# A top-k threshold search whose candidate carries the sign, five masks ahead of the attention, and a rotary swap by transfers

## The chip, the cores and the metric

The program runs on one core of one Trainium2 chip. The core has a matrix engine (TensorE, PE), a vector engine (VectorE, DVE), a scalar engine (ScalarE, ACT), a general engine (GpSimd, POOL) and a queue engine (SyncE, SP); each takes its own instructions in order, and they meet at semaphores. The metric is the device time of one execution in microseconds (us), lower is better. Before the change it is 2630.7 us, the median of 3 runs.

## The reference

One inference step of a two-layer decoder for a prompt of 1024 tokens and 8 sequences of 4 new tokens each (32 tokens, 512 cached ones each), model width 1024. Only the first layer's sparse attention matters here:

```python
def partial_rope(x, cos, sin):           # first 16 of 64 head dims
    x1, x2 = x[..., :8], x[..., 8:16]
    return concatenate([x1 * c - x2 * s, x2 * c + x1 * s, x[..., 16:]])

def attn_project(h, w_in, pos):          # p = h @ w_in, 2120 columns
    q, k, v, qi, ki, wi = split(p, ...)  # q, k, qi, ki get partial_rope

def block(i):                            # 128 queries against 1024 keys
    sc = indexer_scores(qib, wib, ki, valid)   # sum_h relu(qi.ki) * wi
    _, sel = lax.top_k(sc, 256)                # exactly 256 keys a query
    return sparse_attend(qb, k[sel], v[sel])   # softmax over them
```

Every query attends to exactly its 256 best keys (129 of 516 for the sampled tokens), ties going to the earlier key. After it come the output projection, a SwiGLU block, a convolution layer and another SwiGLU block, all untouched by the change.

## The kernel before

Activations are held transposed (features on the 128 partitions, 1056 tokens along the row) and cut into three chunks of 352 tokens. Products are made nearly exact in float32 by splitting each operand into a high and a low part: one tile of a projection (128 output features, 352 tokens) is 24 matmuls, 8 blocks of 128 inputs by three products. The order of all instructions is written out by hand, engine by engine; there is no scheduler. The functions `sp_...`, `pe_...`, `act_...`, `dve_...`, `pool_...` are the programs of the engines, and `x.wait_ge(semaphore, value)` is where one waits for another.

The part in question has four stages.

- **First projection stage** (`pe_proj_a`): five blocks of 3 tiles: the indexer's keys and weights (block 0, 64 or 72 rows), then the indexer's queries. Tile r goes through a chain: PE makes it, ACT evicts it to `psgA` (`act_evac_rope`), PE multiplies it by the permutation `rotm` that exchanges the two halves of each rotated group (`pe_rot`), DVE multiplies that result in PSUM by the sine table into `pafA`, POOL multiplies `psgA` by the cosine table (`pool_cos`), DVE adds (`dve_rope`, counted on `fin_rdy`). `psgA` and `pafA` have two buffers each. POOL also makes the low parts of the weights (`proj_lo`). After tiles 9, 11, 12 and 13 PE turns pages of cached indexer keys (`pe_turn_kx`), which SP has loaded into `xr` by 32 transfers.
- **Index stage**: scores of queries against keys into `s_all`, one row of 384 to 1024 keys for each of the query tiles 2 to 7 (tiles 0 and 1 have no more than 256 keys), and `s_smp` for the 32 sampled tokens.
- **Second projection stage** (`pe_proj_b`), 39 items on PE: 3 tiles of keys, 9 value tiles (`v_tok`), 27 more rotary tiles (1 block of keys, 8 of queries), with a chunk of the modulation weights (`pe_chunks`, about one an item, loaded by SP into a ring of four slots) after each, and the K copy of `pe_turn_k` in nine of them. Here ACT evicts the rotated copy as well (`act_rot`), and POOL does sine product, cosine product and sum (`pool_fin`). At the same time DVE looks for the 256th largest score of every row: a binary search over the bits of a float. One round counts, for seven rows of scores at once, how many values reach the candidate, and sets one bit of the threshold by it. DVE counts five of them, ACT the two longest (1024 and 896 keys) with a Sign activation (`act_count`). Where ACT does so is fixed in its program: the table `COUNT_AT` lays each half round at the middle or end of an item of PE's, by times in which an item counts 10 units (a value item 7).
- **Attention** (`dve_att` and others): 64 pairs (query tile, pair of heads), pair n uses tile n // 8. DVE adds the tile's mask to the scores and takes the row's extreme (`dve_min`), ACT makes the exponential, POOL divides, PE turns and multiplies by the values. The masks of tiles 2 to 7 and of the sampled tokens are made of the thresholds by DVE, six steps each (`dve_mask_step`), 1.5 steps a pair in the first 28 pairs (`dve_masks_at`). Forty chunks of modulation weights are multiplied here as well (`pe_pair_chunks`).

The search before works on magnitudes: a row whose threshold is negative is multiplied by -1 first (`sig`), so that the searched value is positive, and multiplied back at the first step of its mask.

## Time and profile before

| | |
|---|---|
| median of 3 runs | 2630.7 us (2629.48 to 2631.83) |
| the profiled execution, its own time | 2635.32 us |
| its span, first to last instruction | 2633.5 us |
| mean granted TensorE clock | 0.983 |
| busy: PE, DVE, ACT, POOL | 95%, 67%, 42%, 49% |
| chain that ended last, by engine | PE 70%, DVE 11%, DMA 6%, issue 5%, POOL 4%, ACT 2% |
| first projection stage, index stage, second projection stage, attention | about 50 to 131, 131 to 185.6, 185.6 to 382.5, 382.5 to 650 us |

The profiled execution lies 4.6 us above the median, so differences worked out from its rows are taken off the median. The four stages are the first quarter of the kernel; what follows (650 us on) is bound by PE and starts when the attention has ended, so it moves as one block.

In the rows further down a timeline row gives the start in us, the time that the group took in us, the engine (PEld is the load of weights into PE, SPq is SP's queue of transfers), line, operation, what is written from what, the shapes, the number, and in brackets how long the engine had been idle before it and for whom it waited. A row of the stretches view gives for each engine the busy us and the number of instructions, then PE's granted clock as a share of full, the share of the transfer engines, and GB/s. A row of the view by line gives the total busy us, the mean ns of one, and the idle time before.

### The profile page before, as it was taken

What the parts mean: (1) busy time and instruction counts of PE and PEld (TensorE: products, weight loads), DVE (VectorE), ACT (ScalarE), POOL (GpSimd) and SP (SyncE); (2) the same over time, 40 slices, a digit from 0 to 9 for tenths busy, and PEclk for the clock granted to TensorE, in tenths of its full rate; (3) what the DMA queues carried; (4) which work ended last, traced back from release to release, by engine and by line L of the source; (5) the groups of instructions that cost most, each with busy time, mean ns of one, the idle gap of its engine ahead of it and who ended that gap; (6) DMA issues with size and microseconds to landing.
All of it is one profiled execution on the core that took longest, in us unless ns stands there. A gap on an engine that the chain in (4) does not pass through costs nothing.

```text
span 2633.5 us, 51699 instructions
## 1 busy us (share of the span) xinstructions
PE 2512.0 (95%) x20164; PEld 2312.3 (88%) x20164; DVE 1771.3 (67%) x3137; ACT 1101.9 (42%) x2061; POOL 1287.4 (49%) x967
## 2 busy tenths in 40 slices
PE   6979999999998999999999989999989999999999
PEld 4848874677798999999999989999989999999999
DVE  6388888665347756656567687767785665656775
ACT  5155656775235444344212343332454444442223
POOL 3404652344134656566544545545455656654454
PEclk7999999999999999999999999999999999999999
DMA  9205557201433435344894333328334534469731
GB/s 322 78 21 153 177 207 255 70 2 68 129 113 101 146 124 164 117 155 139 328 349 167 117 98 106 107 82 328 117 98 131 164 117 155 139 207 366 278 131 70
DMA packets 316390, 408.00 MB, mean 155 GB/s; under 512 B 40816, under 2 KB 227032, under 8 KB 313338
## 3 DMA queue, kind: packets, MB, share of 16 engines
q1 hardware_dynamic: 316154, 404.75, 45.9%
q8 instruction: 161, 2.64, 0.4%
q14 instruction: 75, 0.61, 0.1%
HBM read 284.85 MB, written 119.85 MB: 154 GB/s over the span
## 4 chain that ended last, share of the span: by engine, by line
PE 70%; DVE 11%; DMA 6%; issue 5%; POOL 4%; ACT 2%; SPq 2%; ACTq 0%; DVEq 0%; POOLq 0%
PE PS L595 10%; PE PS L2492 9%; PE PS L2494 9%; PE PS L2493 9%; PE PS L2553 5%; PE PS L2555 5%; PE PS L2556 5%; PE PS L1855 3%; PE PS L1884 2%; PE PS L1866 2%; POOL ring L2864 2%; DMA t_scratch<-stage 2%; DMA a_scratch<-stage 1%; POOL stage L2877 1%; DVE s_all L1552 1%
## 5 line engine op out<-in xcount | busy, mean ns | idle before, releaser
L2492 PE MATMUL PS<-th,ring 128*128 128x264 f32 x2800 | 800.2, 286 | 19.9 <-DVE y L3007 8.2
L2494 PE MATMUL PS<-th,ring 128*128 128x264 f32 x2800 | 796.8, 285 | 0.0
L2493 PE MATMUL PS<-th,ring 128*128 128x264 f32 x2800 | 795.9, 284 | 0.0
L2492 PEld LDWEIGHTS PS<-th,ring 128*128 128x128 f32 x2800 | 527.8, 189 | 26.8 <-issue 26.1
L2493 PEld LDWEIGHTS PS<-th,ring 128*128 128x128 f32 x2800 | 528.0, 189 | 0.0
L2494 PEld LDWEIGHTS PS<-th,ring 128*128 128x128 f32 x2800 | 527.9, 189 | 0.0
L2864 POOL TENSOR_TENSOR ring<-wraw,ring 128x512 fp32r<-128x512 f32 x232 | 340.3, 1469 | 368.1 <-ACT ring L2648 367.8
L2864 POOL TENSOR_TENSOR ring<-sums,ring 128x512 fp32r<-128x512 f32 x216 | 322.2, 1493 | 276.3 <-ACT ring L2648 276.3
L2553 PE MATMUL PS<-th,ring 128*128 128x264 f32 x1232 | 354.8, 288 | 14.3 <-DVE zs L3196 6.7
L2555 PE MATMUL PS<-th,ring 128*128 128x264 f32 x1232 | 352.9, 286 | 0.0
L2556 PE MATMUL PS<-th,ring 128*128 128x264 f32 x1232 | 352.5, 286 | 0.0
L2648 ACT ACTIVATE ring<-wraw 128x512 fp32r<-128x512 f32 x340 | 211.8, 626 | 299.2 <-PE PS L2556 168.2
L3193 DVE SCALAR_TENSOR_TENSOR y<-PS,mod,y 128x528 f32<-128x528 f32 x308 | 235.0, 766 | 141.2 <-PE PS L2556 128.0
L3007 DVE TENSOR_TENSOR y<-y,PS 128x528 f32<-128x528 f32 x150 | 104.9, 699 | 293.8 <-PE PS L2494 293.6
L2648 ACT ACTIVATE ring<-sums 128x512 fp32r<-128x512 f32 x216 | 136.1, 631 | 353.2 <-PE PS L2494 173.3
L2553 PEld LDWEIGHTS PS<-th,ring 128*128 128x128 f32 x1232 | 234.4, 190 | 16.1 <-issue 11.7
L2556 PEld LDWEIGHTS PS<-th,ring 128*128 128x128 f32 x1232 | 234.7, 191 | 0.0
L2555 PEld LDWEIGHTS PS<-th,ring 128*128 128x128 f32 x1232 | 234.6, 190 | 0.0
L2877 POOL TENSOR_TENSOR stage<-y,stage 128x528 fp32r<-128x528 f32 x110 | 179.2, 1629 | 77.3 <-ACT stage L2668 77.3
L595 PE MATMUL PS<-hhi,uhi 128*128 128x352 f32 (+1 forms) x552 | 189.0, 342 | 14.5 <-DVE hlo L1267 7.3
L2696 ACT ACTIVATE y<-PS 128x528 f32<-128x528 f32 x173 | 105.1, 607 | 186.4 <-PE PS L2494 185.3
L595 PE MATMUL PS<-hhi,ulo 128*128 128x352 f32 (+1 forms) x552 | 180.8, 328 | 0.0
(393 smaller groups left out, 5164.4 us busy)
## 6 DMA issues: line engine op xcount, KB each, us to landing
t_scratch<-stage SPq DMA_DIRECT2D x154, 528.0 KB, 3.3
th<-t_scratch SPq DMA_DIRECT2D x77, 1056.0 KB, 8.7
wraw<-in_ffn_w_gu_dram SPq DMA_DIRECT2D x96, 512.0 KB, 5.2
wraw<-in_ada_w_dram SPq DMA_DIRECT2D x80, 512.0 KB, 4.8
wraw<-in_ffn_w_down_dram SPq DMA_DIRECT2D x80, 256.0 KB, 5.9
wraw<-in_conv_w_in_dram SPq DMA_DIRECT2D x28, 512.0 KB, 5.3
y<-y_scratch SPq DMA_DIRECT2D x12, 1056.0 KB, 8.9
y_scratch<-y SPq DMA_DIRECT2D x6, 2112.0 KB, 7.9
```

What stands on the lines that cost most here:

```text
L595: last = pe.matmul(out, w(kt), x(kt), start=(n == 0), stop=(n == 3 * count - 1))
L2492: pe.matmul(out, hi, x[:, TH, k, :], start=(k == 0 and i in (1, 2, 5)), stop=False, skip_group_check=True)
L2493: pe.matmul(out, hi, x[:, TL, k, :], start=False, stop=False, skip_group_check=True)
L2494: last = pe.matmul(out, lo, x[:, TH, k, :], start=False, stop=(k == 3), skip_group_check=True)
L2553: pe.matmul(out, hi, x[:, TH, 2 * k + s, :], start=(k == 0 and i in (1, 2, 5)), stop=False, skip_group_check=True)
L2555: pe.matmul(out, hi, x[:, TL, 2 * k + s, :], start=False, stop=False, skip_group_check=True)
L2556: last = pe.matmul(out, lo, x[:, TH, 2 * k + s, :], start=False, stop=(k == 1), skip_group_check=True)
L2648: act.activation(slot_of(p)[:, RH, :], split_source(p), ACT.Copy).then_inc(w_hi, 1)
L2696: act.activation(out, result(r, it.groups), ACT.Silu if it.kind == "g" and pos == 6 else ACT.Copy).then_inc(rd_a, 1)
L2864: pool.tensor_tensor(w[:, RL, :], split_source(p), w[:, RH, :].bitcast(F32), ALU.subtract).then_inc(w_lop, 1)
L2877: pool.tensor_tensor(lo.rearrange("p (s n) -> p s n", s=2), token_part(v, i), hi.rearrange("p (s n) -> p s n", s=2), ALU.subtract).then_in ...
L3193: ins = dve.scalar_tensor_tensor(out=out, in0=result(r, BOTH), scalar=gate_of(f, m)[:, 0:1], in1=out, op0=ALU.mult, op1=ALU.add)
```

## The change

It has three parts. (1) The rotary halves are exchanged by transfers from SBUF to SBUF that ACT issues (`act_swap`): four of 8 partitions by 352 numbers a tile (two in block 0), from `psgA` or `psgB` into rows of `pafA` or `pafB` that were set to zero once. PE's 45 products by `rotm` and ACT's 30 evictions of them are gone. (2) The search sets the sign first: one count at 0 gives every row a start of +2 or about -2, the 31 bits below are toggled into `cand` by exclusive or, and there is no separate threshold. The multiplications by the sign before the search and in each mask are gone, and 31 rounds are left of 32. `COUNT_AT` starts at 13 units in place of 24, with 4.8 a half round in place of 4.9. (3) Five of the seven masks (tiles 2, 3, 4, 5, 6, of 384 to 896 keys) are made by DVE ahead of its first instruction of the attention, in `relu` as scratch; the masks of tile 7 and of the sampled tokens follow at pairs 2 to 13, a step a pair.

```diff
-    return [next(s for s, t in enumerate(at) if t >= 24 + 4.9 * h) for h in range(64)]
+    return [next(s for s, t in enumerate(at) if t >= 13 + 4.8 * h) for h in range(62)]
...
         def dve_start(dve):
             dve.memset(ones[:], 1.0)
+            dve.memset(pafA[:], 0.0)
...
-        def pe_rot(pe, r):
-            rows = P if r >= 3 else 64
-            pe.wait_ge(evac, rope_m(r) + 1)
-            after(pe, ts_rdy, r - 1)
-            src = (psgA if r < 15 else psgB)[0:rows, r % 2, :]
-            pe.matmul(rot_bank(r)[0:rows, 0:CH], rotm[0:rows, 0:rows], src, start=True, stop=True).then_inc(rot_mm, 1)
+        def act_swap(act, r):
+
+            act.wait_ge(evac, rope_m(r) + 1)
+            after(act, fin_rdy, r - 1)
+            if r in (15, 16):
+                act.wait_ge(pm_rdy, 1)
+            src, dst = (psgA, pafA) if r < 15 else (psgB, pafB)
+            for head in (0,) if r < 3 else (0, 64):
+                for o in (head, head + 8):
+                    of = 2 * head + 8 - o
+                    act.dma_start(dst[o:o + 8, r % 2, :], src[of:of + 8, r % 2, :]).then_inc(swapped[r % 2], 16)
...
             act.wait_ge(up_mm, UP_END[p] - 2 + n)
-            after(act, rot_mm, r - 1)
+            swap_done(act, r - 2)
             after(act, qc_rdy, r - 1)
...
-        def act_rot(act, r):
-
-            act.wait_ge(rot_mm, r + 1)
-            after(act, fin_rdy, r - 1)
-            act.activation(pafB[:, r % 2, :], rot_bank(r)[:, 0:CH], ACT.Copy).then_inc(ts_rdy, 1)
...
                 for n in range(NCH):
                     act_evac_rope(act, 5, n, psgB)
                     act_count(act, 2 * (ITEM_AT[5] + n))
-                if n:
-                    act_rot(act, R_AT[5] + n - 1)
+                act_swap(act, R_AT[5] + n)
                 act_chunks(act, ITEM_AT[5] + n)
...
-            dve.wait_ge(rot_mm, r + 1)
-            after(dve, fin_rdy, r - 1)
-            dve.tensor_tensor(pafA[0:rows, r % 2, :], rot_bank(r)[0:rows, 0:CH], ropeS[0:rows, chunk(n)], ALU.mult)\
+            if r == 0:
+                dve.wait_ge(const_loaded, 48)
+            swap_done(dve, r)
+            dve.tensor_tensor(pafA[0:rows, r % 2, :], pafA[0:rows, r % 2, :], ropeS[0:rows, chunk(n)], ALU.mult)\
...
+            with dve.Fori(0, ROUNDS) as i:
+                dve.wait_ge(sel, i * 6 + base)
+                count(2, None, ALU.is_ge)
+                dve.wait_ge(cand_rdy, i + 1)
+                signal(count(6, None, ALU.is_lt))
+                count(3, None, ALU.is_ge)
+                count(4, None, ALU.is_ge)
+                signal(count(5, None, ALU.is_ge))
+                dve.wait_ge(sel, i * 6 + (base + 1))
+                dve.wait_ge(sign_cnt, i * NA + NA)
+                signal(dve.tensor_tensor(v(lt, 0, 3), v(cnt, 0, 3), v(kk, 0, 3), ALU.is_gt))
...
             if step == 0:
-                link(dve, dve.tensor_scalar(s, s, bv[0:rows, BS + 3 * E + j:BS + 3 * E + j + 1], None, ALU.mult))
                 link(dve, dve.tensor_scalar(A, s, t, 0.0, ALU.is_gt, ALU.add, accum_out=n))
...
+        MASKS_FIRST, MASKS_LATE = (2, 5, 4, 3, 1), (0, 6)
+
+        def dve_masks_first(dve, entries):
 
+            for j in MASKS_FIRST:
+                for step in range(6):
+                    dve_mask_step(dve, entries, j, step, relu)
             dve.wait_ge(ki_stored, 32)
...
-            for x in range(3 * n // 2, 3 * (n + 1) // 2 if n < 28 else 0):
-                dve_mask_step(dve, entries, (2, 5, 4, 3, 1, 0, 6)[x // 6], x % 6)
+            if 2 <= n < 2 + 6 * len(MASKS_LATE):
+                dve_mask_step(dve, entries, MASKS_LATE[(n - 2) // 6], (n - 2) % 6, mscr)
```

ACT in the second projection stage, the first two tiles of block 10, before (L1005 is the eviction, L900 a count, L1012 the eviction of the rotated copy, L828 the high part of a weight, L1026 the K copy):

```order
L1005 ACTIVATE psgB<-PS 128x352
L900 ACTIVATE junkA,bv<-s_all,bv 128x896
L1012 ACTIVATE pafB<-PS 128x352
L828 ACTIVATE uhi<-wraw 128x1024
L1026 ACTIVATE ktok<-PS 128x256
L900 ACTIVATE junkA,bv<-s_all,bv 128x1024
L1005 ACTIVATE psgB<-PS 128x352
L900 ACTIVATE junkA,bv<-s_all,bv 128x896
L1012 ACTIVATE pafB<-PS 128x352
L1026 ACTIVATE ktok<-PS 128x256
```

and the same two tiles after the change (L1000, L906, L827 and L1016 are the same statements under new line numbers, L855 is the swap):

```order
L1000 ACTIVATE psgB<-PS 128x352
L906 ACTIVATE junkA,bv<-s_all,bv 128x1024
L855 DMA pafB<-psgB 8x352 x4
L827 ACTIVATE uhi<-wraw 128x1024
L1016 ACTIVATE ktok<-PS 128x256
L906 ACTIVATE junkA,bv<-s_all,bv 128x896
L1000 ACTIVATE psgB<-PS 128x352
L906 ACTIVATE junkA,bv<-s_all,bv 128x1024
L855 DMA pafB<-psgB 8x352 x4
L1016 ACTIVATE ktok<-PS 128x256
```

The copy of the tile before (one activation) has given way to the swap of this tile (four transfers, issued by ACT in its own order).

DVE at the end of a round of the search, before (`junkC` is the count of the sampled tokens, 128x5 the five rows that DVE counts):

```order
L1600 TENSOR_SCALAR junkC,bv<-s_smp,bv 32x516
L1660 REGISTER_ALU
L1636 TENSOR_TENSOR PS<-bv,PS 128x5
L1662 REGISTER_ALU
L1638 TENSOR_SCALAR PS<-PS,bv 128x5
L1664 REGISTER_ALU
L1640 SCALAR_TENSOR_TENSOR bv<-PS,bv 128x5
L1645 TENSOR_TENSOR bv<-bv,PS 128x5
L1647 REGISTER_ALU
```

and after the change, from the wait for ACT's counts to the end of the round:

```order
L1626 TENSOR_TENSOR PS<-bv,PS 128x3
L1627 REGISTER_ALU
L1628 ISA
L1628 TENSOR_SCALAR PS<-bv 128x4
L1629 REGISTER_ALU
L1630 TENSOR_SCALAR PS<-PS,bv 128x3
L1631 REGISTER_ALU
L1632 ISA
L1632 SCALAR_TENSOR_TENSOR bv<-PS,bv 128x4
L1634 REGISTER_ALU
L1635 SCALAR_TENSOR_TENSOR bv<-PS,bv 128x3
L1616 REGISTER_ALU
```

Before, a round had eight small instructions, four for ACT's two rows among the counts and four for the others behind them; now it has five, all behind the last count.

DVE behind the search, before (L1682 is the last step of the search, L1942 the first of the attention):

```order
L1680 TENSOR_TENSOR PS<-PS,bv 128x2
L1681 TENSOR_TENSOR bv<-bv,PS 128x2
L1682 TENSOR_TENSOR bv<-bv 128x7
L1942 ISA PbS,bv<-PS,cneg 128x128
L1942 ISA bv 128x1
```

and after the change, the first of the five masks (35 instructions in all, then the attention):

```order
L1655 TENSOR_TENSOR bv<-bv,PS 128x2
L1666 TENSOR_SCALAR relu,bv<-s_all,bv 128x384
L1668 TENSOR_SCALAR bv<-bv 128x1
L1669 TENSOR_SCALAR relu<-s_all,bv 128x384
L1671 SCALAR_TENSOR_TENSOR relu<-relu 128x384
L1673 SCALAR_TENSOR_TENSOR relu<-relu,bv 128x384
L1675 SCALAR_TENSOR_TENSOR relu<-s_all,bv,relu 128x384
L1677 TENSOR_SCALAR masks<-relu 128x384
```

## Rows read from the trace of the kernel before

**Rows 1.** Stretches: second projection stage and first 28 pairs, busy us of each engine.

```profile
185.60:382.50 196.90, 194.72 (x1344) 162.53 (x1344) 175.76 (x636) 111.58 (x223) 101.75 (x96) 0.98 0.51 158
...
382.50:475.00 92.50, 82.92 (x767) 41.27 (x768) 74.61 (x233) 56.11 (x200) 29.05 (x57) 0.94 0.78 260
```

**Rows 2.** PE's timeline: a tile without a rotation behind it, and rotations.

```profile
236.64 0.43 PE L595 MATMUL PS<-hhi,uhi 128*128 128x352 f32 x1
...
241.23 0.43 PE L595 MATMUL PS<-hhi,uhi 128*128 128x352 f32 x1
...
353.57 0.75 PE L849 MATMUL PS<-psgB,rotm 128*128 128x352 f32 x2
...
358.74 0.75 PE L849 MATMUL PS<-psgB,rotm 128*128 128x352 f32 x2
```

**Rows 3.** Timeline at the end of the first projection stage.

```profile
125.99 0.46 ACT L1005 ACTIVATE psgA<-PS 128x352 f32<-128x352 f32 x1 [4.43 <-PE PS L595]
...
127.21 0.63 DVE L1098 TENSOR_TENSOR qiT<-qcA,pafA 128x352 f32<-128x352 f32 x1
...
127.47 2.57 POOL L834 TENSOR_TENSOR ulo<-wraw,uhi 128x1024 fp32r<-128x1024 f32 x1
...
128.41 2.01 DVE L1098 TENSOR_TENSOR qiT<-qcA,pafA 128x352 f32<-128x352 f32 x1
```

**Rows 4.** The pages in `xr`: SP's queue, landing, PE's loads (ns; first and last start).

```profile
77.16 19.18 SPq L777 DMA_DIRECT2D xr<-in_cache_kidx_dram  x16
...
DMA to landing us min/median/max: 1.6/1.8/11.5
...
L924 PEld LDWEIGHTS PS<-ident,xr x16: 140/141/143, 102.1 to 121.7; 128*128 128x128 f32 x16
```

**Rows 5.** DVE's timeline, from the index stage into the search.

```profile
187.66 1.22 DVE L1600 TENSOR_SCALAR_CACHE_REDUCE junkA<-s_all 128x1024 bf16<-128x1024 f32 x1
...
193.22 0.53 DVE L1610 TENSOR_SCALAR PS<-bv 128x1 f32<-128x1 f32 x7
...
199.37 0.61 DVE L1600 TENSOR_SCALAR_CACHE_REDUCE junkB<-s_all,bv 128x384 bf16<-128x384 f32 x1
```

**Rows 6.** DVE's timeline, one round of the search.

```profile
231.56 0.61 DVE L1600 TENSOR_SCALAR_CACHE_REDUCE junkB<-s_all,bv 128x384 bf16<-128x384 f32 x1
...
235.66 0.17 DVE L1636 TENSOR_TENSOR PS<-bv,PS 128x5 f32<-128x5 f32 x1
...
236.54 0.61 DVE L1600 TENSOR_SCALAR_CACHE_REDUCE junkB<-s_all,bv 128x384 bf16<-128x384 f32 x1
```

**Rows 7.** Groups by line and shape of ACT, second projection stage.

```profile
L900 ACT ACTIVATE junkA<-s_all,bv 128x1024 bf16<-128x1024 f32 x32 | 36.8, 1150 | 41.0 <-DVE bv L1640 41.0
...
L900 ACT ACTIVATE junkA<-s_all,bv 128x896 bf16<-128x896 f32 x32 | 33.1, 1033 | 0.0
...
L828 ACT ACTIVATE uhi<-wraw 128x1024 fp32r<-128x1024 f32 x8 | 8.3, 1054 | 0.0
...
L1026 ACT ACTIVATE ktok<-PS 128x256 f32<-128x256 f32 x8 | 3.1, 382 | 0.5 <-DMA out_dram<-ktok 0.5
```

**Rows 8.** SP's queue: a small transfer at the start.

```profile
4.58 0.30 SPq L635 DMA_DIRECT2D vst<-in_c_prompt_dram  x1
```

**Rows 9.** Timeline from the last round to the attention.

```profile
373.84 0.18 DVE L1670 SCALAR_TENSOR_TENSOR bv<-bv 128x2 f32<-128x2 f32 x1
...
384.18 0.29 DVE L1942 CUSTOM_DVE_ANT_0 PbS<-PS,cneg 128x128 f32<-128x128 f32 x1
...
382.97 0.49 PE L1855 MATMUL PS<-kT,hhi 64*128 64x128 f32 x4 [0.54 <-ACT mod L889]
```

**Rows 10.** Groups by line and shape: two of the masks' instructions.

```profile
L1699 DVE TENSOR_TENSOR_SCAN mscr<-mscr 128x896 f32<-128x896 f32 x1 | 2.0, 2025 | 0.0
...
L1705 DVE TENSOR_SCALAR masks<-mscr 128x384 bf16<-128x384 f32 x1 | 0.4, 360 | 0.0
```

**Rows 11.** Waits in the first 28 pairs: who waited for whom.

```profile
PE PS L1866 <- POOL PbS L2023: 3.3, 5, 1.2
```

More of the change, by code:

```diff
@@ L893, in act_count @@
         def act_count(act, half):
-            for h in range(64):
+            for h in range(62):
                 if COUNT_AT[h] == half:
@@ L1018, in act_proj_a @@
                         act_evac_rope(act, p, n, psgA)
+                    act_swap(act, 3 * p + n)
                 proj_hi(act, p + WR)
@@ L1616, in dve_select @@
-            link(dve, ins)
-            for j, (s, rows, L, k) in enumerate(entries):
-                if j < NA:
-                    dve.tensor_scalar(ka[:, j:j + 1], one(kk, j), -2.0, float(L), ALU.mult, ALU.add)
-                dve.tensor_scalar(s, s, one(sig, j)[0:rows], None, ALU.mult)
-            ins = dve.memset(v(cand), 2.0)
+            ins = dve.tensor_tensor(v(cand), v(cand), v(th), ALU.add)
             link(dve, ins)
```

168 lines of the change are left out of this document (66 added, 102 removed).

## The prediction, written before the changed kernel ran

> **What bounds the kernel now.** I read the chain that ended last first: 70% PE, 11% DVE. The change touches only the first quarter, so I followed the chain there by stage. In both projection stages it is made of PE's tiles; the stretches view gives PE 194.7 busy of 196.9 us in the second one, and DVE 175.8 beside it [rows 1]. So two things run side by side from 185.6 on: PE's 39 items, and DVE's search, whose 32 rounds end at 373.8, followed by a closing part until 384.18. PE had its first scores under way at 382.97 and waited for DVE [rows 9]. **The attention starts when the later of the two is done, and before the change they are level within about a microsecond**: to gain, both must become shorter, and what is put on DVE ahead of the attention counts in full once DVE is the later. In the first 28 pairs PE is idle 92.5 - 82.9 = 9.6 us [rows 1], 3.3 of it named as POOL, which waits for DVE, busy with masks [rows 11].
>
> **First projection stage.** A rotation costs PE what an item with one takes above one without: 358.74 - 353.57 = 5.17 against 241.23 - 236.64 = 4.59, so 0.58 us [rows 2]. Fourteen of the fifteen rotations of this stage lie ahead of its end: 14 x 0.58 = 8.1 us off PE. Two things give some back.
> The pages in `xr` come from SP, which waits for nothing here that moves: its last transfer is issued by 77.16 + 19.18 = 96.34 and lands 1.8 later, at 98.1 [rows 4]. PE turned the first page at 102.1 [rows 4]; nine rotations earlier this is 96.9, so PE waits 1.2 us.
> The tail: the eviction of tile 14 started at 125.99, the sum of its rotary parts ended at 128.41 + 2.01 = 130.42, 4.4 us later [rows 3]. Now: eviction 0.46, four issues on ACT, the landing, DVE's product and sum. I find no transfer issued by ACT here; the nearest row is SP's of 8 partitions, 0.30 [rows 8]; I add 0.05 between two (an estimate), so 1.4 for four. Landing 1.8 [rows 4]. The last product could then start 3.7 us after the eviction began. But rows 3 show a sum of two SBUF operands taking 2.01 us and ending 0.4 after POOL's 2.57 us split ended (127.47 + 2.57 = 130.04), where the same sum took 0.63 just before it: DVE with two SBUF operands waits for POOL. The product used to read PSUM; now it reads SBUF twice and can wait too. POOL's split follows ACT's high part, which stands behind the four issues: 0.4 + 1.4 + 1.05, so it lies at 2.9 to 5.4, and product and sum end at 5.4 + 0.5 + 0.65 = 6.6. The tail grows 2.2 us (0.5 if the product gets in first).
> The Trainium skill (SBUF — State Buffer, "SBUF: two separate sides") says the port pair is an exclusive lock between a DVE operation with two SBUF inputs and a GpSimd one; by it the tail is the 6.6, which this case's 2.01 us sum agrees with.
> Stage gain: 8.1 - 1.2 - 2.2 = 4.7. The index stage moves as a block; none of its instructions change.
>
> **The search, from the start of the second projection stage (185.6).** Setup: seven counts at 187.66 to 193.2, then 6.2 us of sign factors until the first round at 199.37 [rows 5]. After: the same counts and about ten instructions of one to seven numbers, 0.07 to 0.17 each, 1.2 us in all. 5.0 us less; rounds could begin 8.8 after the stage's start.
> A round: 236.54 - 231.56 = 4.98 when it waits for nothing; 4.1 to 235.66 are five counts and what is done among them, 0.88 the last four small steps [rows 6]. Taking the four small steps of ACT's rows out from among the counts leaves 3.6 for these, and the new chain of five, two of them side by side, is some 0.65: 4.25 a round. But ACT's two counts stand at fixed places in PE's items, so DVE can't outrun PE: 9.6 units a round, an item of 10 units taking 4.59, or 4.8 with a K copy. PE paces the search.
> PE's stage: 196.9 - 30 x 0.58 = 179.5. By `COUNT_AT` the last half round (61) lies at 305.8 units, in item 33; behind this item's tile come five items and a chunk, 5 x 4.59 + 0.8 = 23.8, so the tile ends at 155.7. With eviction 0.4, count 1.03 [rows 7] and 0.8 for DVE's last steps: 158.
> **Does ACT keep up?** An item now: eviction 0.4, counts (1.15 + 1.03) x 10/9.6 = 2.3, K copy 0.38, a third of a high part 0.35 [rows 7], together 3.4; four issues 1.4; sum 4.8, against 4.6 to 4.8 for PE. That is level. Bounds: at no cost for an issue ACT has 1.2 us to spare; at 0.6, twice rows 8, it has 5.8 and is late by 1.2 an item. I take 0.35 because a swap is nearest in shape to the 8-row transfer of rows 8, and 1.5 us of lateness over some twenty rotary items that carry counts: last round at 159.5. Before it ended 373.8 - 185.6 = 188.2 after the start.
> A page has a price where no row has one: the Trainium skill (DMA: Bandwidth & Descriptors, "Anatomy of one DMA — SWDGE (gpsimd) path") puts the sequencer's own part of a transfer at about 50 ns. By it ACT would never be late and the end would come 1.5 us earlier than my sum; no run here shows it yet.
> Where the swap is late, POOL waits: it needs it only behind the next tile's cosine product, an item later, so 4.6 us cover 1.4 of issue, 1.8 of landing and a count of 1.15. Without the cover each late microsecond reaches ACT's eviction two tiles on.
>
> **Behind the search.** Closing part: 384.18 - 373.84 = 10.3 [rows 9]; the same eight passes over the two longest rows, one small step less: 10.2. Then the five masks, 35 instructions, the longest the scan of 896 keys, 2.03, the shortest of full width the last step of 384 keys, 0.36 [rows 10]; by shape, without the sign product, 3.7 + 4.5 + 5.4 + 6.1 + 6.9 = 26.7, and 0.04 between each and the next makes 28.1. DVE is ready at 159.5 + 10.2 + 28.1 = 197.8, where it was 384.18 - 185.6 = 198.6: a gain of 0.8. PE is done 18 us earlier than that and idles. The search's 29 us are eaten by the masks; PE's 17 us in this stage are hidden.
> **Attention.** It starts 4.7 + 0.8 = 5.5 earlier. In it POOL's 3.3 go, and some of the rest, since the queries and the first chunks have landed long before; two masks remain in pairs 2 to 13, one with a scan of 1024 keys, longer than that of rows 10, and take some back. I take 3.5 (bounds 0 and 9.6). The clock is left out: in this stage it was granted at 0.94 before [rows 1], and PE idles ahead of it in both kernels, now longer, which is one more reason not to take more.
> **Sum**: 5.5 + 3.5 = 9.0 off the profiled 2635.3, so off the median: 2630.7 - 9.0 = **2621.7 us**. What differs by under 0.2% (5.3 us) this measurement can't tell from no change.
>
> **Rivals.**
> *A, ACT hardly notices the swaps* (issues run beside its counts, and the product gets in ahead of POOL): 1.5 and 1.7 less, and more of the 9.6: some 2616. For it: waits and issues aren't counted as busy on any engine. Chance 0.25; the forecast itself 0.36.
> *B, ACT becomes the bound.* Its program is in order: counts, eviction and four issues; at 0.5 us an issue an item takes 5.4, 0.8 more than PE's, over twenty items 16 us in place of 1.5: 2636, slower. It decides from 1.5 + 9 us of lateness, 0.5 an item, some 0.45 an issue on. Against it: SP's 0.30; for it: SP does nothing else than issue, ACT's case isn't measured. Chance 0.18.
> *C, masks and sums wait for POOL.* The masks ahead run beside POOL's rotary work; fifteen of their 35 instructions read SBUF twice, as the sum of rows 3 did. At 0.45 us each (an estimate, a quarter of the 1.63 that the sum of rows 3 waited) it is 7 us: 2628, no change. Chance 0.14.
> *D, late landings.* The slowest landing in rows 4 is 11.5 us, with the queue full; ACT's swaps share the transfer engines, 51% busy in this stage [rows 1]. Ten swaps late by 2 us are 20 us: 2640. Against it: median 1.8. Chance 0.05.
> *E, nothing moves*: ACT level but attention gives nothing, 2626. Chance 0.02.
> From these: forecast and A 0.61 faster (a few of their cases fall short of 5.3, some of C beyond it), same 0.17, slower 0.22. Low end: A with all of the 9.6, 2612. High end: B, between its 2636 and 2644 at 0.6 us an issue: 2640.
>
> **What the profile of the changed kernel would show.** PE tiles of 3.8 us back to back in the first stage, a wait for `xr` of about 1 us at the first page; relu's last activation near 180.9 in place of 185.6; rounds of 4.4 to 4.6; ACT's queue with issues of about 0.35 and no idle time before its counts; PE ready some 18 us before DVE's first instruction of the attention, near 378.7; few waits for POOL behind it. Wrong would be: issues above 0.45; rounds of 5 or more; DVE's masks stretched beside POOL; an attention that takes as long as before.

## The result and the profile after

The changed kernel takes **2653.4 us** (median of 4 runs, 2650.3 to 2656.8), the kernel before beside it 2631.3 us (2629.5 to 2635.0): a ratio of 1.0073, 95% interval 1.0051 to 1.0095 (the ratio is the measurement's own estimate over all runs; the two medians alone give 1.0084). By the medians it is 22 us slower, where I forecast 9 us faster; the time lies above the high end of my range. The profiled execution took 2656.81 us (span 2655.0, mean granted clock 0.975 in place of 0.983).

The chain that ended last, shares of the span by engine; PE had 70% before, and issue 5%:

```profile
PE 62%; DVE 11%; issue 8%; DMA 6%; POOL 5%; SPq 3%; ACT 3%; ACTq 1%; DVEq 0%; POOLq 0%
```

Stretches from the end of the index stage to DVE's first minimum of the attention, and the 93 us behind it; they answer to [rows 1]:

```profile
182.40:401.20 218.80, 179.97 (x1288) 153.78 (x1288) 190.56 (x551) 100.18 (x192) 107.58 (x99) 0.92 0.53 166
401.20:494.20 93.00, 88.76 (x789) 44.59 (x790) 47.10 (x186) 57.51 (x203) 27.94 (x56) 0.89 0.68 221
```

The stage that I wanted at 197.8 us up to DVE's readiness takes 218.4. PE's busy time in it did fall, from 194.7 to 180.0 us: the rotations are gone. But PE is hardly earlier. Who PE and DVE waited for in this stretch (us in total, times, longest):

```profile
PE PS L1831 <- DVE bv L1918: 22.5, 1, 22.5
PE PS L868 <- DMA wraw<-in_ada_w_dram: 8.7, 5, 3.6
PE PS L594 <- ACT ktok L1016: 5.8, 8, 1.3
```

```profile
DVE PS L1626 <- ACT junkA L906: 10.4, 12, 2.5
```

PE's tiles of the stage end hardly sooner after its start than before (its first scores at 378.43 lie 195.6 us after 182.8; before, 382.97 lay 197.4 after 185.6; my working had 179.5), and then it stands 22.5 us until DVE is ready. ACT's transfers, from the view of their line (min/median/max in ns, first and last start):

```profile
L855 ACTq DMA_DIRECT2D pafB<-psgB x120: 631/632/1536, 189.1 to 376.2; - x120
```

An issue takes 0.632 us of ACT's queue, twice the 0.30 of [rows 8]. What that does depends on where it stands. ACT's timeline, one item of the K stretch:

```profile
304.80 1.15 ACT L906 ACTIVATE junkA<-s_all,bv 128x1024 bf16<-128x1024 f32 x1 [0.38 <-DVE bv L1635]
304.86 1.29 ACTq L855 DMA_DIRECT2D pafB<-psgB  x2
...
306.18 1.29 ACTq L855 DMA_DIRECT2D pafB<-psgB  x2
307.59 1.06 ACT L827 ACTIVATE uhi<-wraw 128x1024 fp32r<-128x1024 f32 x1 [1.55 <-PE PS L594]
308.56 0.37 ACT L1016 ACTIVATE ktok<-PS 128x256 f32<-128x256 f32 x1
308.82 1.03 ACT L906 ACTIVATE junkA<-s_all,bv 128x896 bf16<-128x896 f32 x1
...
309.85 0.45 ACT L1000 ACTIVATE psgB<-PS 128x352 f32<-128x352 f32 x1
```

The first count of a round runs at 304.80, two issues start right beside it, two more follow, then a high part and a K copy, and only at 308.82 comes the second count of the same round. The whole swap stands between a round's two counts. DVE's timeline, one round from 347.47 and, from 352.44, the last one, answers to [rows 6]:

```profile
347.47 0.61 DVE L1593 TENSOR_SCALAR_CACHE_REDUCE junkB<-s_all,bv 128x384 bf16<-128x384 f32 x1 [0.41 <-issue]
...
351.08 0.15 DVE L1626 TENSOR_TENSOR PS<-bv,PS 128x3 f32<-128x3 f32 x1
351.31 0.23 DVE L1628 TENSOR_SCALAR PS<-bv 128x4 int32<-128x4 f32 x1
351.44 0.22 DVE L1630 TENSOR_SCALAR PS<-PS,bv 128x3 int32<-128x3 f32 x1
351.68 0.22 DVE L1632 SCALAR_TENSOR_TENSOR bv<-PS,bv 128x4 int32<-128x4 int32 x1
351.82 0.21 DVE L1635 SCALAR_TENSOR_TENSOR bv<-PS,bv 128x3 int32<-128x3 int32 x1
352.44 0.61 DVE L1593 TENSOR_SCALAR_CACHE_REDUCE junkB<-s_all,bv 128x384 bf16<-128x384 f32 x1 [0.41 <-issue]
...
357.12 0.82 DVE L1641 SCALAR_TENSOR_TENSOR PS<-bv 128x2 f32<-128x2 f32 x1
```

Five small steps take 0.95 us bare, and the next count starts 0.41 us after them. The round from 347.47 waited for nothing, and the pitch to the next one is 4.97, what it was before. Then DVE's row from the closing part, the first instruction of the first two masks, and the attention's first (it was at 384.18, [rows 9]):

```profile
359.40 1.86 DVE L1650 TENSOR_TENSOR relu<-relu,s_all 128x1024 f32<-128x1024 f32 x1
...
369.25 0.61 DVE L1666 TENSOR_SCALAR_CACHE_REDUCE relu<-s_all,bv 128x384 f32<-128x384 f32 x1
...
375.60 0.75 DVE L1666 TENSOR_SCALAR_CACHE_REDUCE relu<-s_all,bv 128x512 f32<-128x512 f32 x1
...
401.20 0.29 DVE L1918 CUSTOM_DVE_ANT_0 PbS<-PS,cneg 128x128 f32<-128x128 f32 x1
```

| from the profiled executions | before | forecast | after |
|---|---|---|---|
| second projection stage starts (relu ends) | 185.6 | 180.9 | 182.8 |
| from there to the first round | 13.8 | 8.8 | 8.6 |
| from there to the last round's end | 188.2 | 159.5 | 174.2 |
| closing part | 10.3 | 10.2 | 12.2 |
| masks ahead | 0 | 28.1 | 32.0 |
| DVE's first minimum | 384.2 | 378.7 | 401.2 |
| from it to the first minimum of 640 keys | 104.2 | 100.7 | 103.2 |
| all, own time | 2635.3 | 2626.3 | 2656.8 |

The attention starts 17.0 us later, its stretch up to the first minimum of 640 keys is 1.0 shorter, and 5.5 more are lost behind that: PE ran at half clock once more in the output projection. PE's windows of the changed kernel (busy, count, clock, transfers' share, GB/s):

```profile
381.00:401.00 20.00, 0.00 (x0) 0.50 0.44 164
401.00:420.00 19.00, 15.96 (x100) 0.50 0.43 140
420.00:440.00 20.00, 18.86 (x174) 0.95 0.82 265
690.00:703.00 13.00, 12.34 (x88) 0.57 0.45 125
```

At 0.5 the clock is at its lower level, 1.2 GHz. It stayed there from PE's idle stretch until about 420, for 19 us of work; before, 384 to 394 had 0.62 and 394 to 404 had 0.87. After 690, behind a stretch in which PE's work has gaps in both kernels, it fell once more; before it did not.

Neither loss of clock can be put down to the longer idle time, though. The second fall is there in kernels in which PE never idled long ahead of the attention, here the kernel of e12 below, and so are 5.5 us behind the first minimum of 640 keys: that remainder was 2147.0 us before, 2152.4 in the changed kernel, and 2140.5 to 2156.1 in the experiments below (e1 2140.5, e12 2152.8, e8 2156.1; e5 left out). So what follows the attention did not move quite as one block.

```profile
670.00:690.00 20.00, 17.19 (x113) 0.66 0.44 123
```

And the low clock around the attention's start ended 9 to 14 us behind its first minimum in the kernel before and in eleven of the experiments, 21 in the changed kernel, and 23 to 24 in e1, e4 and e7. In e13 PE had idled 24.6 us ahead of it, more than the changed kernel's 22.5; in e1 and e4 it had waited for DVE 1.3 and 0.7 us.

### The profile page after: what moved, and what is told of

It reads as the page before. It is cut to its first block, busy times and chain, and to the rows that moved or that the text cites. A ratio compares the mean times of both kernels' runs of the same rounds, so it can differ in the third digit from the quotient of the medians.

```text
span 2655.0 us, 51486 instructions
## 1 busy us (share of the span) xinstructions
PE 2491.5 (94%) x20074; PEld 2301.6 (87%) x20074; DVE 1768.7 (67%) x3001; ACT 1089.5 (41%) x2027; POOL 1294.2 (49%) x968
## 3 DMA queue, kind: packets, MB, share of 16 engines
q8 instruction: 160, 2.62, 0.4%
## 4 chain that ended last, share of the span: by engine, by line
PE 62%; DVE 11%; issue 8%; DMA 6%; POOL 5%; SPq 3%; ACT 3%; ACTq 1%; DVEq 0%; POOLq 0%
PE PS L2468 9%; PE PS L2470 8%; PE PS L2469 8%; PE PS L2529 5%; PE PS L2531 5%; PE PS L2532 5%; PE PS L594 4%; PE PS L1831 3%; PE PS L1860 3%; DMA t_scratch<-stage 3%; PE PS L1842 2%; POOL ring L2840 2%; POOL stage L2853 2%; DMA a_scratch<-stage 1%; PE PS L2490 1%
## 5 line engine op out<-in xcount | busy, mean ns | idle before, releaser
L2468 PE MATMUL PS<-th,ring 128*128 128x264 f32 x2800 | 800.3, 286 | 22.5 <-DVE y L2983 8.0
L594 PE MATMUL PS<-hhi,uhi 128*128 128x352 f32 (+1 forms) x552 | 187.7, 340 | 20.5 <-DVE hlo L1257 7.4
L2672 ACT ACTIVATE y<-PS 128x528 f32<-128x528 f32 x173 | 105.2, 608 | 188.2 <-PE PS L2470 187.7
```

What stands on the lines that cost most here:

```text
L594: last = pe.matmul(out, w(kt), x(kt), start=(n == 0), stop=(n == 3 * count - 1))
L2468: pe.matmul(out, hi, x[:, TH, k, :], start=(k == 0 and i in (1, 2, 5)), stop=False, skip_group_check=True)
L2672: act.activation(out, result(r, it.groups), ACT.Silu if it.kind == "g" and pos == 6 else ACT.Copy).then_inc(rd_a, 1)
```

## The experiments

The search alone and the swap alone are the changed lines of one part put into the kernel before, or taken back out of the changed one. Masks are moved by one line, shown for e4 and e14:

```diff
-        MASKS_FIRST, MASKS_LATE = (2, 5, 4, 3, 1), (0, 6)
+        MASKS_FIRST, MASKS_LATE = (), (2, 5, 4, 3, 1, 0, 6)      # e3, e4, e9, e15
+        MASKS_FIRST, MASKS_LATE = (2,), (5, 4, 3, 1, 0, 6)       # e14
```

with 1.5 steps a pair inside the attention, from pair 0 on as before the change (in e14, and in e10 with its two masks ahead, from pair 2 on). The count table is one number:

```diff
-    return [next(s for s, t in enumerate(at) if t >= 13 + 4.8 * h) for h in range(62)]
+    return [next(s for s, t in enumerate(at) if t >= 13 + 4.96 * h) for h in range(62)]
```

Each experiment ran beside the kernel before (2634.6 to 2635.7 us there; 2631.3 beside the changed kernel). Differences in us between two experiments are taken from their ratios. "Start" is DVE's first minimum in the profiled execution, 384.2 before.

| | swap | new search | masks ahead | COUNT_AT | start | ratio, 95% |
|---|---|---|---|---|---|---|
| e1 | yes | no | 0 | as before | 377.6 | 0.9998, 0.9988 to 1.0009 |
| e3 | no | yes | 0 | 13 + 4.8 h | 383.2 | 0.9990, 0.9979 to 1.0001 |
| e2 | no | yes | 5 | 13 + 4.8 h | 398.4 | 1.0045, 1.0028 to 1.0063 |
| e4 | yes | yes | 0 | 13 + 4.8 h | 380.7 | 0.9993, 0.9980 to 1.0005 |
| changed kernel | yes | yes | 5 | 13 + 4.8 h | 401.2 | 1.0073, 1.0051 to 1.0095 |
| e9 | yes | yes | 0 | 13 + 4.96 h | 370.4 | 0.9955, 0.9940 to 0.9971 |
| e14 | yes | yes | 1 | 13 + 4.96 h | 371.5 | 0.9956, 0.9942 to 0.9970 |
| e13 | yes | yes | 5 | 13 + 4.96 h | 395.0 | 1.0036, 1.0023 to 1.0048 |
| e15 | no | yes | 0 | 13 + 4.96 h | 384.4 | 0.9990, 0.9975 to 1.0005 |

**First set: each part alone.** Theories: ACT's issues (I), against the search's rounds and the bare masks (L).

> The kernel before with the rotation by four small transfers a tile alone; search, COUNT_AT and masks are those of before. What the changed kernel's trace showed: first stage 3.2 us shorter (relu's last start 182 in place of 185.6), each issue 0.64 us on ACT, PE's second stage no shorter than before (379.2 - 182.4 = 196.8). Theory I (ACT's issues, 2.6 us a tile, hold up PE through its K copies and the search through ACT's counts): PE's items of the K stretch 5.2 to 6.1 us, rounds 5.3 us in the mean, attention starts at 378 to 382, time 2624 to 2630, so about no change. Theory L (issues hardly matter, the loss of 22 us comes from the search's rounds and the masks): PE's items 4.6 to 4.8 throughout, PE ready by 366, attention starts when the search ends, 182.4 + 13.8 + 32 x 4.98 + 10.3 = 366 to 368, time about 2614.

> The kernel before with the new search and the five masks ahead, the rotation left on PE. Theory L (a round of the new search takes 4.97 us on DVE as before, closing 12.2, masks 32 bare): rounds end near 185.6 + 9 + 31 x 5.05 = 351, attention starts at 395, eleven us later than before, time 2641 to 2646 (the upper end if PE's idle stretch costs clock again behind it). If the round were really 4.25 us and only ACT's issues had hidden it, rounds would follow PE's items (9.6 units of 0.517 = 4.96 a round), the same end: this run can't tell those two apart, its round without a wait for ACT can: 4.97 or 4.25. If the masks ahead were the gain that I had forecast behind the search (few waits for POOL, 3.5 us), the stretch from the first pair to the first mask of 640 keys falls from 104.2 to about 100.7.

> The kernel before with the new search alone: rotation on PE, all seven masks inside the attention as before, in the same order and rhythm. DVE ready 351 + 12.2 = 363, PE at 383: the attention starts with PE, at 383. Expected by theory L: time within 2 us of before (2630), DVE idle some 20 us ahead of the attention. A gain of over 4 us would say that DVE's small work in the attention got cheaper (the sign product gone), a loss that the new search costs something outside its own place.

> The changed kernel with none of the masks ahead of the attention: all seven inside it, in the rhythm of before. DVE ready at 357.0 + 12.2 = 369.2, PE at 379.2: the attention starts at 379.5, 22 us earlier than in the changed kernel. If the masks ahead are the whole loss: 2653.4 - 22 + 1 = 2632, and another 5 less if the stretches of half clock (401 to 420 and 690 to 703 in the changed kernel) go with PE's long idle: 2627. If it stays above 2640, something that I haven't named costs.

The masks carry the loss: e2 (2646.8 us, 0.8 above the range expected for it) against e3 starts 15.2 us later, the changed kernel against e4 20.5, and the times follow (0.55% and 0.80%, 14.5 and 21 us). The swap alone brings nothing, though it starts the attention 6.6 us earlier; the search alone brings nothing that can be told from no change.

Theory I, as I had put it, did not hold: in e1, with the same 0.632 us issues, PE's items of the K stretch take 4.8 to 5.1 us but for one of 6.0, not the 5.2 to 6.2 of the changed kernel. ACT in e1:

```profile
292.34 1.15 ACT L906 ACTIVATE junkA<-s_all,bv 128x1024 bf16<-128x1024 f32 x1
...
293.49 0.44 ACT L1000 ACTIVATE psgB<-PS 128x352 f32<-128x352 f32 x1
293.83 1.03 ACT L906 ACTIVATE junkA<-s_all,bv 128x896 bf16<-128x896 f32 x1
293.96 1.29 ACTq L855 DMA_DIRECT2D pafB<-psgB  x2
...
295.28 1.29 ACTq L855 DMA_DIRECT2D pafB<-psgB  x2
296.68 0.38 ACT L1016 ACTIVATE ktok<-PS 128x256 f32<-128x256 f32 x1 [1.72 <-issue]
```

Here the swap stands between the second count of one round (293.83) and the first of the next. That is where I then looked.

Part of e1's 6.6 us went with the clock. PE had waited 7.3 us for a chunk of weights just ahead of the attention, and the 20 us behind:

```profile
380.00:400.00 20.00, 17.10 (x104) 0.50 0.80 271
```

Its stretch of the first pairs took 107.7 us, 3.5 more than before. The rest of the 6.6 is not found in this trace, which was the fastest of e1's 12 runs (2625.8 against a median of 2634.2). The mean clock of the 12 was 0.979, that of the 29 runs of before 0.983, and among those 29 a clock lower by 0.001 went with 1.24 us more (correlation 0.79 in size): by that slope, an estimate, the difference is some 5 us.

**Second set: issues, the candidate's place, SP's queue.** Edits against e4:

```diff
# e5: each transfer of 8 rows as two of 4
+                    for q in (0, 4):
+                        act.dma_start(dst[o + q:o + q + 4, r % 2, :], src[of + q:of + q + 4, r % 2, :])
# e6: the step on the rows that ACT counts stands ahead of the last two counts
+                signal(dve.tensor_tensor(v(lt, 0, 3), v(cnt, 0, 3), v(kk, 0, 3), ALU.is_gt))
                 count(4, None, ALU.is_ge)
...
# e7: a step's chunks of weights ahead of its stores
-                    sp_chunks(sp, lo, lo + 3)
+                    sp_chunks(sp, lo, hi if p > 8 else lo + 3)
```

> The changed kernel without masks ahead (e4), but each swap of 8 rows made as two of 4 rows: eight issues a tile, the same bytes. Theory I (ACT pays by the issue, 0.64 us each): 5.1 us of issues a tile, an ACT item of 3.4 + 5.1 = 8.5 less about 1.2 that runs beside its counts, so items of some 7 us in the K stretch and rounds near 7 us there; over 27 rotary items that carry counts 2 us and more each on e4's 5.2: 2675 to 2700. If ACT pays by rows or bytes (an issue of 4 rows 0.32 us), nothing changes against e4's 2633.

Ratio 1.0291 (1.0274 to 1.0307), 2712.4 us, beyond what I expected. The issues of 4 rows:

```profile
L856 ACTq DMA_DIRECT2D pafB<-psgB x240: 584/585/617, 210.9 to 455.8; - x120
```

Half the bytes cost 0.585 us in place of 0.632: ACT pays nearly all of it by the issue. All 348 are 204 us of ACT's queue, where e4's 174 were 110: 94 us more, and 79 us came out in the time; the first stage alone grew by some 20 us (relu's last start at 203.7).

> e4 with the round's small steps in the places that they had before the change: the decision for the two rows that ACT counts (and the samples' row) between the fourth and last counts, not behind all five. Theory C (the new round gives ACT its candidate at its very end; ACT then stands in order ahead of its count, 35.4 us in e4, and evictions, K copies and swaps stand behind it, which stretches PE's items of the K stretch to 5.1 to 6.2 us, while the search of before with the same swaps had 4.8): ACT's waits for DVE under 20 us, K items 4.8 to 5.0, rounds 4.8 to 4.9, DVE through its closing part by 362 to 365 (369 in e4). PE's end gains 3 to 5 of its 12 lost unless loads hold it; time 2628 to 2632. Theory I (it is the issues as such): items stay at 5.2 to 6.2, time as e4.

A miss: ratio 1.0043 (1.0025 to 1.0061), 13 us slower than e4. Rounds of the K stretch took 5.8 to 7.1 us. DVE's timeline, two rounds of it, the decision on ACT's rows:

```profile
272.43 0.17 DVE L1624 TENSOR_TENSOR PS<-bv,PS 128x3 f32<-128x3 f32 x1 [0.90 <-ACT junkA L906]
...
279.53 0.17 DVE L1624 TENSOR_TENSOR PS<-bv,PS 128x3 f32<-128x3 f32 x1 [2.19 <-ACT junkA L906]
```

With the decision early, DVE stands still for ACT's second count with two counts of its own still to do, where in e4 it does them meanwhile. So the path candidate, first count, swap, second count, decision is the loop that sets the round, and e6 put more of DVE's work on it. The late candidate was not the fault.

> e4 with SP's order changed: the weight chunks of a step ahead of its query stores, and the nine stores of v_tok spread in threes behind the weights of three steps, not in one block of 5.0 us ahead of loads. Theory Q (PE without its rotations runs into SP's queue: 8.3 us of waits for wraw in e4, 11.4 in e1, 2.1 before the change): waits for wraw under 3, PE's items 14 and 15 at 5 to 6 in place of 6.8 and 7.5, PE ready some 5 us earlier, attention 3 to 5 us earlier, 2628 to 2631. If it is the transfers' bandwidth and not the queue's order, waits stay.

A miss too: ratio 0.9994 (0.9981 to 1.0006), no change. PE's waits for `wraw` fell only from 8.3 to 6.9 us, and its first scores came 1.5 us earlier. PE waited instead for ACT's last copy for the modulation (5.6) and, past its first scores, for POOL's last sum (3.4). The queue's order was not what held it.

> e6 and e7 together, no masks ahead. PE ready at about 368, DVE at about 364, attention from 368 to 370, 14 us earlier than before the change, if both theories hold. What the clock takes back: e1 and e4 had a mean granted clock of 0.979 and 0.981 over their runs, before 0.983, and among runs of one kernel 0.001 of clock goes with 1.3 to 1.6 us. Time 2620 to 2626; the time at the same clock as before would be 2617 to 2620.

Ratio 1.0027 (1.0014 to 1.0040), 2643.1 us: a third miss, e6's loss stays.

**Third set: the place of the counts.** In which items the two counts of rounds 14 to 18 stand (items and rounds counted from 0), by the table (a: behind the eviction, ahead of the swap; b: behind the swap):

```
before, e1           18b-19a  19b-20a  20b-21a  21b-22a  22b-23a
changed, 13 + 4.8 h  17a-17b  18a-18b  19a-19b  20a-20b  21a-21b
e9, 13 + 4.96 h      17b-18a  18b-19a  19b-20a  20b-21a  21b-22a
```

> e4 with one number changed: COUNT_AT at 13 + 4.96 h units in place of 13 + 4.8 h. By the table, from item 16 to item 27 the changed kernel has both of a round's ACT counts inside one item, the first ahead of the tile's swap and the second behind it; in the kernel before and in e1 the first stands at an item's end and the second ahead of the next item's swap. With 4.96 no item from 12 on has both. Theory P (the four issues, 2.6 us, stand between the two counts of one round and so on the path candidate, counts, decision, candidate): rounds 4.97 from the fourth on in place of 5.2 to 6.2, K items 4.8 to 5.0, DVE's last round starts at 347 to 349 (352 to 354 in e4), DVE ready by 363, PE's start of the attention then set by its own tail (queries' last tiles) at 374 to 378; time 2627 to 2631. Theory I (ACT has simply too much work, wherever it stands): rounds stay at 5.2 to 6.2 in the K stretch and the time at e4's 2633.

It held, and by more than I had expected: 2624.3 us, ratio 0.9955, 10 us faster than e4 by one number, and 12 faster than before (11 by the medians). Both sides came earlier: PE's first scores at 369.5 (379.8 in e4), DVE ready at 362.8 (370.4 in e4). Some 2 us of each lie ahead of the search, in the first stage of these two executions; the changed kernel, whose search began at the same time as e9's (191.4), had PE at 378.4 and DVE's closing part done at 369.2. K items took 4.8 us, and DVE's waits for ACT in the search were (10.4 in the changed kernel):

```profile
DVE PS L1626 <- ACT junkA L906: 5.5, 5, 2.4
```

ACT's timeline, one item in 4.7 us. The order is that of e1; the high part that the item shown above had is not in this one:

```profile
307.56 1.14 ACT L906 ACTIVATE junkA<-s_all,bv 128x1024 bf16<-128x1024 f32 x1
...
308.69 0.45 ACT L1000 ACTIVATE psgB<-PS 128x352 f32<-128x352 f32 x1
309.04 1.04 ACT L906 ACTIVATE junkA<-s_all,bv 128x896 bf16<-128x896 f32 x1
309.17 1.29 ACTq L855 DMA_DIRECT2D pafB<-psgB  x2
...
310.49 1.29 ACTq L855 DMA_DIRECT2D pafB<-psgB  x2
311.89 0.37 ACT L1016 ACTIVATE ktok<-PS 32x256 f32<-32x256 f32 x1 [1.72 <-issue]
```

Like with like, three items in a row with the same instructions, from first count to first count, the middle one with the high part: 4.6, 5.9 and 4.6 us here, 5.9, 6.2 and 5.2 in the changed kernel. The changed kernel's own rounds show the same: of those with both counts in one item, the ones in the K stretch (15 to 24) took 5.1 to 6.2 us from start to start; the last five, whose counts stand apart again and which have no K copies beside them, took 4.97. The new table also slows the pace from 9.6 to 9.92 units a round. No run moves the counts by half an item at the old pace, so place and pace are told apart only by these traces, where the swap between the counts is seen and DVE's waits for ACT fall with it.

> The changed kernel with COUNT_AT as in e9, SP's order as in e7, and two of the five masks ahead (384 and 512 keys, 11.9 us) in place of five. DVE ready at 363 + 12 = 375, about where PE is; the attention then starts at 375 to 378, 7 to 9 us before that of the kernel before, with two masks less inside it. Without the clock that is 2622 to 2625; with what the clock took in e1, e4 and e7 (2 to 5 us) 2625 to 2630. Above 2633 would say that masks inside the attention were free and those ahead never pay.

2628.8 us, ratio 0.9968 (0.9956 to 0.9981): within the expectation, not better than e9. DVE was ready at 376.2, 5.6 us after PE, so the second mask was bare.

> The changed kernel as it is, with 76 matmuls of the identity by itself into a PSUM bank that nobody reads (76 x 0.27 = 20.7 us), placed on PE behind its last product of the second projection stage, where it idles 22.5 us for DVE. They add work and change no result. Theory G (the loss behind 401 is the clock: 0.50 granted from PE's idle stretch to about 420): the granted clock is 1.0 through 380 to 420, DVE's ninth minimum comes 10 to 11 us behind the first but the seventeenth at 21 in place of 23.4, mean clock of the runs 0.980 or more in place of 0.975, time 2 to 6 us below the changed kernel's 2653.4 against 2631.3: ratio 1.005 to 1.0065. Rival (clock and idling have nothing to do with each other, or the time behind 401 is set by DVE): ratio 1.0073 as before, or a little more, if the dummy work runs late into the attention's start.

The edit, behind PE's last product of the stage:

```diff
             pe_ada_turned(pe, SG_W - 1)
+            for _ in range(76):
+                pe.matmul(bank[3][:, 0:P], ident[:], ident[:], start=True, stop=True)
```

Ratio 1.0052 (1.0037 to 1.0067), mean clock of the runs 0.981. The windows that had 0.50 and 0.50:

```profile
381.00:401.00 20.00, 14.76 (x130) 0.96 0.34 131
401.00:420.00 19.00, 16.13 (x122) 0.68 0.56 176
```

PE still idled 5 us at the end and fell again, for less long. The seventeenth minimum came 21.2 us behind the first, not 23.4, but the stretch up to the first minimum of 640 keys took 103.0 us, hardly less than the 103.2. The time fits my expectation; the clock that I had expected, 1.0 through 420, did not come. Whether the run gained anything is open, since the two intervals overlap, and the higher mean clock says little: over half of the rise is the filled idle time itself, which the profile counts at its granted 0.96 in place of 0.50. The fall behind 690 was there again (0.62 from 690 to 703).

> The kernel before with the new search, rotation left on PE, and three of the five masks ahead (384, 512 and 640 keys, 18 us), which fit in front of PE's end: DVE ready at 363 + 18 = 381, PE at 383. Attention starts at 383 with PE never idle ahead of it, and has four masks in place of seven inside. If masks inside cost the attention time, its first 28 pairs lose part of their 9.6 idle us: time 2624 to 2630, against e3's 2632.2 beside 2635.7. If not, it is e3's ratio, 0.999.

Ratio 0.9990 (0.9981 to 1.0000), start 382.8, as e3: three masks hidden beside PE cost nothing and bring nothing that can be measured.

**Fourth set: what was still open.**

> The changed kernel with COUNT_AT at 13 + 4.96 h, the five masks ahead kept. Theory: each part adds up; DVE ready at e9's 363.5 + 32 = 395.5, attention 25 us later than in e9 (370.4), of which the attention gives back some 3 for having fewer masks inside (changed kernel against e4: start 20.5 us apart, times 0.80% or 21 us apart, so rather 0) and the clock takes some 3. Ratio 0.9955 + 0.0095 = 1.004 to 1.006, 5 us below the changed kernel's 1.0073. If the phase had nothing to do with the search's end: 1.0073.

Ratio 1.0036: the count table is worth 0.37%, about 10 us, in the changed kernel as well, and the masks cost 0.81% on top of e9, 21 us for a start 24.6 later (the stretch of the first pairs fell from 103.4 to 99.7). PE idled 24.6 us ahead of the start, and the clock was back sooner than in the changed kernel all the same:

```profile
405.00:414.00 9.00, 8.30 (x83) 0.92 0.86 308
```

So five masks fewer inside do shorten the attention, by 3.7 us here and by 2.2 in e2 against e3, and what the changed kernel lacked of it goes with the longer low clock (0.90 in the mean of that stretch, 0.94 here).

> e9 with the mask of 384 keys ahead (5.9 us), six inside. DVE ready at 363.5 + 6 = 369.5, PE at 369.5: the mask is hidden beside PE's tail. Expected: e9's ratio of 0.9955, give or take 0.001; if masks inside the attention cost, 1 to 2 us better. Above 0.9975 would say that a mask costs even where it is hidden.

Ratio 0.9956, as e9. The mask's last step, and DVE's first minimum, which then waited for PE:

```profile
368.62 0.36 DVE L1677 TENSOR_SCALAR masks<-relu 128x384 bf16<-128x384 f32 x1
371.54 0.29 DVE L1918 CUSTOM_DVE_ANT_0 PbS<-PS,cneg 128x128 f32<-128x128 f32 x1 [2.56 <-PE PS L1831]
```

> e3 (new search, rotation on PE, no masks ahead) with COUNT_AT at 13 + 4.96 h: the control for theory P. Without the swap's issues nothing long stands between a round's two counts, and PE's 5.2 to 5.4 us items pace the stage: attention starts at 383 as in e3, ratio 0.999 as e3's. A gain like e9's (0.4%) here would say that the table was bad in itself and the swap innocent.

Ratio 0.9990, start 384.4, as e3: without the swap's issues the table makes no difference.

## Why the prediction was wrong

In the order of its steps; the forecast's DVE ready at 378.7 against 401.2 makes 22.5 us.

- **First stage**: forecast 4.7, measured 2.8 in these two executions. (One pair is a rough measure: relu's last start lay at 183.1 to 187.0 in the five kernels with the rotation on PE and at 180.6 to 183.9 in the eleven with the swap of four issues, 2.4 apart in the mean.) PE's wait for the pages, taken at 1.2, was this:

```profile
PE PS L930 <- DMA xr<-in_cache_kidx_dram: 4.4, 1, 4.4
```

  The pages came at 96.8, 1.3 ahead of my sum, but PE stood there at 92.4, not 96.9; 1.3 us of that are a stage that happened to begin earlier (48.28 in place of 49.54). What the sum had at nothing is what the wait does to the clock. Behind it:

```profile
96.80:103.00 6.20, 6.20 (x27) 0.64 0.94 293
```

  Before, PE ran these items at 1.00. From the first page to tile 14's eviction it took 23.2 us, against 23.9 with the five rotations: of their 2.9 us 0.7 were left.

  The tail grew as forecast in kind, by 3.3 and not 2.2, 1.2 of it since four issues took 2.62. DVE's sine product did wait for POOL's split, here side by side:

```profile
124.39 2.71 DVE L1078 TENSOR_TENSOR pafA<-pafA,ropeS 128x352 f32<-128x352 f32 x1 [1.75 <-DMA pafA<-psgA]
```

```profile
124.38 2.34 POOL L833 TENSOR_TENSOR ulo<-wraw,uhi 128x1024 fp32r<-128x1024 f32 x1 [2.88 <-ACT uhi L827]
```

  The product of two SBUF operands takes 0.53 alone. By the Trainium skill (SBUF — State Buffer, "SBUF: two separate sides") a DVE operation with two SBUF inputs and a GpSimd one that reads SBUF lock each other out of a shared port pair. The trace agrees: the product took 2.71 us and ended 0.4 behind POOL's split.
- **Setup of the search**: right, 8.6 against 8.8.
- **A round of 4.25 us**: wrong, 4.97. The four small steps do leave the counts (3.61 in place of 4.1), but the chain behind them is 0.95, not 0.65, and a gap of 0.41 stands at the loop's turn (0.12 before). That is worth 3.4 us here, since I had PE pace the rounds at 4.6 to 4.8: DVE's own pace is slower than that.
- **"That is level"**: the step that failed most. Rounds had a mean of 5.37, 12 us over their floor in all, where I had 1.5 of lateness; in e9 they had 5.18, 6 us over it. So 6 of the 12 are the swap between the counts. The other 6 stood at nothing in my sum: they lie in the first two rounds and beside items 12 to 15, in two of which PE waited 3.1 us for its weights. My 0.35 us an issue was 0.63, above the 0.45 from which I had rival B decide, and B was named at 0.18. But B's working, a sum of ACT's work in an item, is not what happened either: e9 has the same issues and the same work, and its K items take 4.8 us. By that sum it is 3.4 + 4 x 0.632 = 5.9; two of the four issues run beside the count ahead of them (1.0 to 1.15 us), which leaves 4.8 to 4.9. What counts is whether the 2.6 us lie between a round's two counts, which `COUNT_AT` decides; I read from the change only when the last half round comes, not what stands between the halves. The listing of ACT's order that stands ahead of the prediction has it: count, swap, count. e9, e13 and the control e15 show what it costs.
- **Closing part**: 12.2 against 10.2. Its two passes over two SBUF operands took 1.86 and 1.72 us beside POOL, where the same passes over the same rows took 1.23 and 1.09 before, POOL being idle beside the second and for part of the first. That is 1.3 of the 2.0; the rest is in the small steps, of which the first took 0.82 in place of 0.18.
- **The masks**: 32.0 against 28.1. That DVE's time here counts in full was right and e2, e3, e4, e13 and e14 show it; so was rival C's mechanism, closing part and masks together at most 5.9 us over my sum where I priced it 7. It had to be added to the forecast, not held against it. The step that made it fatal stands ahead of this: the 29 us that the search was to free were 14. That makes 1.9 of the 22.5 for the first stage, -0.2 for the setup, 14.9 for the rounds, 2.0 for the closing part and 3.9 for the masks.
- **Late landings** (rival D) were small: POOL waited 13.2 us for swaps in 11 waits, the longest 2.7. How much of it reached PE no run separates.
- **Attention 3.5 us shorter**: the mechanism was right (e13 against e9 3.7; e2 against before 4.4, of which e3 has 2.2 without any mask moved), but in the changed kernel only 1.0 was left, with PE at half clock for its first 21 us (until 13 before, 10 in e2).
- **"The clock is left out"**: wrong by omission, but a longer idle time isn't the whole of it. 2.5 us were missing in the attention and 5.5 behind it, both in stretches of half clock. That the longer idle time caused them is not shown: e13, idling longer, had the low clock until only 12 us behind its start, and the later fall stands in e12, e9 and e15 as well. The 5.5 us lie inside the scatter between profiled executions and may be bad luck. Without them the kernel is slower all the same, since its attention starts 17.0 us later.

The Trainium skill gives about 50 ns as the sequencer's part of a transfer on GpSimd's path (DMA: Bandwidth & Descriptors, "Anatomy of one DMA — SWDGE (gpsimd) path"). The swaps go by ACT's queue, so the figure was not for this case, and it doesn't fit it: ACT's queue was held 0.632 us for 8 rows and 0.585 for 4. I had kept it out of the sum, and rightly, but my row was SP's, and it was off by two as well.

Left open: why the same loop body turned in 0.12, 0.26, 0.32 or 0.41 us in four kernels, what sets how long the clock stays low behind the attention's start (9 to 14, 21 or 24 us), and how much of the loss behind the attention returns in every run.

## What to carry to other kernels

Where a loop runs over two engines, what counts is the work that stands between its two ends in program order, not the sum of work: after a change to either side, list what lies between the halves again, and expect a table tuned for the old pitch to be off. A cost that an engine pays per issue is to be read from a row of that engine, and small transfers are to be counted by issues. Work put ahead of a barrier is free only as far as the other side is later than DVE: one mask fitted beside the swap (e14) and three without it (e12), five cost 21 us. None of the masks that fitted brought time. And before a stretch of low clock is blamed on a change, look for it in kernels without the change.

## What the runs showed of the hardware that I had not expected

- A transfer issued by ACT holds its queue 0.632 us with 8 rows of 1408 bytes and 0.585 with 4, against 0.30 for SP's 8-row one; two of them can start beside an activation under way (304.80 and 304.86 above).
- DVE's loop turned in 0.12 us (before), 0.26 (e1, same loop), 0.32 (e2, e3) and 0.41 (changed kernel, same loop as e3); a round without waits was 4.97, 5.12, 4.87 and 4.97.
- TensorE's granted clock stood at 0.50 for the first 21 us of the attention in the changed kernel and until 9 to 24 us behind its start in the others, in no order of PE's wait for DVE ahead of it (24.6 us in e13 and back after 12, 1.3 us in e1 and back after 23); a wait of 4.4 us (first page) was followed by 0.64 over 6.2 us.
- Between runs of one kernel the time followed the mean clock, 1.24 us for 0.001 in the 29 runs of before. With a correlation of 0.79 that is the larger part of their scatter (2630.0 to 2641.4).
